# The opening of a two-model kernel: modulation blocks as columns on TensorE, three of them on VectorE, and a paired first projection

## The reference, cut to what matters

```python
s_c = jax.nn.silu(c)
s_cc = jax.nn.silu(c_ctx)[None]
ml = (s_c @ w_mod[i] + b_mod[i]).reshape(-1, 3, 3, D)       # shift, scale, gate of three stages
h = gated_residual(h, ml, 0, swiglu(ada_in(h, norm_g[i, 0], ml, 0), ffn_w_in[i, 0], ffn_w_out[i, 0]), 0.5)
...
mc = (s_cc @ w_mod[i] + b_mod[i]).reshape(-1, 3, 3, D)
hc = gated_residual(hc, mc, 0, swiglu(ada_in(hc, norm_g[i, 0], mc, 0), ffn_w_in[i, 0], ffn_w_out[i, 0]), 0.5)
```

## Time and profile before

| | |
|---|---|
| median of 3 runs | 3142.65 us (3140.11 to 3145.58) |
| the profiled execution | 3145.35 us |
| its span, first to last instruction | 3143.5 us |
| TensorE busy | 3055.1 us, 97% |
| VectorE busy | 1778.6 us, 57% |
| ScalarE busy | 1177.8 us, 37% |
| mean granted clock of TensorE | 0.982 |
| HBM read | 417.30 MB, 133 GB/s |

### The profile page before, as it was taken

How to read it: one execution, slowest core, us unless ns; L and a number is a source line. 1 busy time by engine, 2 the same in 40 slices (tenths; PEclk the granted TensorE clock), 3 DMA queues, 4 the chain that set the end, 5 groups by cost and what they waited for, 6 DMA issues and landing times. The chain is left out here.

```text
span 3143.5 us, 46965 instructions
## 1 busy us (share of the span) xinstructions
PE 3055.1 (97%) x19451; PEld 2711.1 (86%) x19451; DVE 1778.6 (57%) x3279; ACT 1177.8 (37%) x2025; POOL 86.6 (3%) x132
## 2 busy tenths in 40 slices
PE   7999999999999999999999998999999999999998
PEld 3788889888888888888888878999898999899998
DVE  1667675435449886653333544556656665656665
ACT  2322224333343222232222444444544544454443
POOL 1000000000000000000000110000001000001000
PEclk9899999999999999999999999999999999999999
DMA  9346543122135566632423332656335454435452
GB/s 279 95 144 184 144 148 105 51 88 94 61 94 162 168 201 184 184 94 74 114 79 98 99 100 75 191 169 191 107 115 181 151 185 132 138 98 168 148 183 87
DMA packets 509004, 421.46 MB, mean 134 GB/s; under 512 B 18234, under 2 KB 505962, under 8 KB 508792
## 3 DMA queue, kind: packets, MB, share of 16 engines
q1 hardware_dynamic: 505752, 412.33, 43.0%
q0 software_dynamic: 3040, 6.13, 0.8%
HBM read 417.30 MB, written 1.12 MB: 133 GB/s over the span
## 5 line engine op out<-in xcount | busy, mean ns | idle before, releaser
L1387 DVE TENSOR_TENSOR w_low<-raw,w_high 128x1024 fp32r<-128x1024 f32 (+2 forms) x720 | 762.8, 1101 | 327.0 <-ACT w_high L925 325.8
L925 ACT ACTIVATE w_high<-raw 128x1024 fp32r<-128x1024 f32 (+2 forms) x720 | 648.2, 949 | 613.3 <-PE gemm L2042 360.5
L2042 PE MATMUL gemm<-xh,w_high 128*128 128x512 f32 (+1 forms) x1904 | 689.1, 362 | 6.8 <-DVE xl L1425 6.2
L2042 PE MATMUL gemm<-xl,w_high 128*128 128x512 f32 (+1 forms) x1904 | 681.0, 358 | 0.0
L2042 PE MATMUL gemm<-xh,w_low 128*128 128x512 f32 (+1 forms) x1904 | 681.0, 358 | 0.0
L2042 PEld LDWEIGHTS gemm<-xh,w_high 128*128 128x128 f32 x1904 | 359.3, 189 | 67.4 <-DVE xl L1425 6.9
L2042 PEld LDWEIGHTS gemm<-xh,w_low 128*128 128x128 f32 x1904 | 359.2, 189 | 57.6
L2042 PEld LDWEIGHTS gemm<-xl,w_high 128*128 128x128 f32 x1904 | 359.6, 189 | 55.3 <-issue 0.2
L2042 PE MATMUL gemm<-yh,w_high 128*128 128x256 f32 x1216 | 354.0, 291 | 12.8 <-DVE yl L1450 7.1
L2042 PE MATMUL gemm<-yl,w_high 128*128 128x256 f32 x1216 | 347.1, 285 | 0.0
L2042 PE MATMUL gemm<-yh,w_low 128*128 128x256 f32 x1216 | 346.9, 285 | 0.0
(11 more groups left out here) (331 smaller groups left out, 4278.0 us busy)
## 6 DMA issues: line engine op xcount, KB each, us to landing
raw<-in_ffn_w_in SPq DMA_DIRECT2D x176, 512.0 KB, 5.2
raw<-in_w_mod SPq DMA_DIRECT2D x72, 1024.0 KB, 7.1
raw<-in_w_in SPq DMA_DIRECT2D x50, 1024.0 KB, 5.3
raw<-in_w_up SPq DMA_DIRECT2D x32, 1024.0 KB, 5.5
raw<-in_w_down SPq DMA_DIRECT2D x32, 1024.0 KB, 5.2
raw<-in_ffn_w_out SPq DMA_DIRECT2D x32, 768.0 KB, 4.4
raw<-in_ret_w_in SPq DMA_DIRECT2D x24, 1024.0 KB, 5.2
raw<-in_ffn_w_out SPq DMA_DIRECT2D x32, 640.0 KB, 4.1
```

The source lines that it names most:

```text
L925: act.activation(wh[i % SPL][:, a:b], raw[slot_of["w", i]][:, a:b], ACT.Copy).then_inc(w_high, 1)
L1387: dve.tensor_tensor(wl[slot][:, a:b], raw[slot][:, a:b], wh[i % SPL][:, a:b].bitcast(F32), ALU.subtract).then_inc(w_low, 1)
L2042: ins = pe.matmul(out, l_, r_, start=first and j == 0, stop=last and j == 2)
```

## The change

The first stage's twelve modulation blocks are done in another way, and the opening's work is put in another order.

- The order of loads becomes 0, 8, 1, 2, (x, ctx), 9, 3, 4, 10, 5, 6, 7, and block 11 goes between the weight blocks. `MOD0` is 8: blocks 0 to 7 are TensorE's, blocks 8, 9, 10 (the first part of the gate) are done in the opening by VectorE with `sum_mod`, block 11 too, during the first projection.
- TensorE's blocks are done as columns: the raw block's 128 x 128 parts are the stationary operand and silu(c), silu(c_ctx) the two moving columns, 16 matmuls a block. The rows, their copies by ScalarE and the turns are gone; VectorE takes eight pairs of columns and the bias in one instruction. The T5 product goes to another PSUM bank.
- On TensorE the order is blocks 0, 1, 2, T5 product, transposes of x, then blocks 3 to 7 with the three additions over partitions between them, then the sums of squares and the spread.
- ScalarE does the decay and lambda work before the copies of `h`, then the squares, then the high part of weight block 0, then the root.
- `scales(0)` and `gates(0)` are apart: the gate is made after `in000`.
- The first projection is `wide`.

```diff
-MOD0 = 12
+FIRST_MODS = (0, 8, 1, 2, 9, 3, 4, 10, 5, 6, 7)
+MOD1 = len(FIRST_MODS)
+MOD0 = MOD1 - 3
...
-        seq = [("m", b) for b in range(MOD0)]
+        seq = [("m", b) for b in FIRST_MODS]
         mod_after = {}
-        spans = ((G["in000"].s0, G["ret_qk0"].s0, MOD0, 36), (G["in010"].s0, G["in100"].s0, 36, 72))
+        spans = ((G["in000"].s0 + 3, G["ret_qk0"].s0, MOD1, 36), (G["in010"].s0, G["in100"].s0, 36, 72))
...
             act.activation(sc[:, :, 1], vecB[:, VB["c_ctx"]:VB["c_ctx"] + 8], ACT.Silu).then_inc(c_silu, 1)
-            for b in range(4):
-                act.wait_ge(chunk_mod, b + 1)
-                act.activation(mrow[:, b % 4, :], bank[b % 4][0:2, 0:WB], ACT.Copy).then_inc(mod_row, 1)
-            for c in range(DC):
-                act.wait_ge(x_turned, c + 1)
-                act.activation(h[:, c, :], aux[c % 4][:, :], ACT.Copy).then_inc(h_init, 1)
...
             act.activation(lam[:, 4:8], lam[:, 0:4], ACT.Exp).then_inc(lam_exp, 1)
-            for b in range(4, MOD0):
...
+            for c in range(DC):
+                act.wait_ge(x_turned, c + 1)
+                act.activation(h[:, c, :], aux[c % 4][:, :], ACT.Copy).then_inc(h_init, 1)
+            N = norms["n00"]
+            for c in range(DC):
+                square(N, c)
+            splits_upto(0)
+            roots(N)
+            highs(N, 0, 4)
+            splits_upto(1)
+            highs(N, 4)
...
+            def take_columns(q):
+
+                n = min(8, 2 * MOD0 - 8 * q)
+                dve.wait_ge(chunk_mod, 4 * q + n // 2)
+                dve.tensor_tensor(mod[:, 8 * q:8 * q + n, :], bank[q][:, 0:2 * n].rearrange("p (c v) -> p c v", v=2),
+                                  vecA[:, 8 * q:8 * q + n].unsqueeze(2).to_broadcast([P, n, 2]),
+                                  ALU.add).then_inc(mod_out, 1)
...
+            dve.wait_ge(c_silu, 2)
+            sum_mod(MOD0)
             dve.wait_ge(small_in, 80)
-            take_rows(0)
...
-            for q in range(1, MOD0 // 4):
-                take_rows(q)
...
-            coefficients(0)
+            dve.wait_ge(t5_g, 1)
+            dve.tensor_copy(gt5[:, :], bank[3][0:8, :]).then_inc(t5_row, 1)
+            sum_mod(MOD0 + 1)
+            take_mod(MOD0)
+            sum_mod(MOD0 + 2)
+            take_mod(MOD0 + 1)
+            for q in range(2):
+                take_columns(q)
+            dve.wait_ge(mod_out, 2)
+            dve.wait_ge(mod_taken, 2)
+            scales(0)
+            N = norms["n00"]
+            inverses(N)
+            steps = pieces_of(N)
+            splits_upto(0)
+            for _ in range(4):
+                next(steps)
+            splits_upto(1)
+            run(steps)
+            take_mod(MOD0 + 2)
...
                     run(gemm(f"in{l}{f}{s}"))
+                    if l + f + s == 0:
+                        take_mods(12)
+                        gates(0)
+                        dve.wait_ge(coef_ready, 1)
...
-                    for m in range(n, n + 4):
+                    for m in range(n, n + 4) if n else ():
                         wait_chunk_out(pe, m - 4)
...
+            def mod_columns(b):
+
+                slot = slot_of["m", b]
+                pe.wait_ge(raw_in[slot], value_of["m", b])
                 for j in range(2):
                     o = 4 * (b % 4) + 2 * j
-                    ins = pe.matmul(aux[q % 2][:, o:o + 2], mrow[:, b % 4, P * j:P * j + P], ident[0:2, 0:2],
-                                    start=True, stop=True)
...
+                    for k in range(DC):
+                        at = WB * k + P * j
+                        ins = pe.matmul(bank[b // 4][:, o:o + 2], raw[slot][:, at:at + P], sc[:, k, :], start=k == 0,
+                                        stop=k == DC - 1)
                 ins.then_inc(chunk_mod, 1)
...
-            for b in range(4):
-                mod_rows(b)
-                if b:
-                    mod_turn(b - 1)
-            mod_turn(3)
+            for b in range(3):
+                mod_columns(b)
             pe.wait_ge(pool_ready, 5)
             pe.wait_ge(small_in, 80)
-            pe.matmul(aux[3][0:8, :], tab[:, :], hot[:, :], start=True, stop=True).then_inc(t5_g, 1)
+            pe.matmul(bank[3][0:8, :], tab[:, :], hot[:, :], start=True, stop=True).then_inc(t5_g, 1)
             pe.wait_ge(x_in, 64)
...
             pe.wait_ge(h_init, 8)
-            for b in range(4, MOD0):
-                mod_rows(b)
...
+            add_partitions(MOD0)
+            mod_columns(3)
+            mod_columns(4)
+            add_partitions(MOD0 + 1)
+            mod_columns(5)
+            mod_columns(6)
+            add_partitions(MOD0 + 2)
+            mod_columns(7)
+            N = norms["n00"]
+            for c in range(DC):
+                mean_square(N, c)
+            spread(N)
+            pe.wait_ge(mod_out, 2)
+            pe.wait_ge(t5_row, 1)
...
-                        run(gemm(f"in{l}{f}{s}", normed(f"n{l}{j}"), wide=s == 0 and G[f"in{l}{f}{s}"].n0 > 0))
+                        run(gemm(f"in{l}{f}{s}", normed(f"n{l}{j}"), wide=s == 0))
```

More of the change, by code:

```diff
@@ L178, in program @@
                                ("gt5", [8, 512], F32), ("tab", [33, 8], F32),
-                               ("hot", [33, 512], F32), ("mrow", [2, 4, WB], F32)])[7:]
-        xrows, vrows, lamv, lamp, rpbp, gt5, tab, hot, mrow = xrows
+                               ("hot", [33, 512], F32)])[7:]
+        xrows, vrows, lamv, lamp, rpbp, gt5, tab, hot = xrows
         qr = xt
@@ L598, in program @@
         raw_in = [sem(f"raw_in{i}") for i in range(RAW)]
-        chunk_mod = sem("mod_row_in_psum")
-        mod_row = sem("mod_row")
-        mod_cols = sem("mod_cols")
+        chunk_mod = sem("mod_columns_in_psum")
         mod_out = sem("mod_out")
@@ L1167, in _ @@
             act.activation(lam[:, 4:8], lam[:, 0:4], ACT.Exp).then_inc(lam_exp, 1)
-            for b in range(4, MOD0):
[L1169 to L1172, removed]
+            for c in range(DC):
[9 more added lines that the diff above has]
+            highs(N, 4)
             def ffn(l, f, j):
-                if norms[f"n{l}{j}"]["halves"] == 1:
+                if norms[f"n{l}{j}"]["halves"] == 1 and l + f:
                     norm(f"n{l}{j}")
@@ L1179, in ffn @@
                     run(gemm(f"out{l}{f}{s}"))
-            splits_upto(1)
             act.wait_ge(rpb_out, 16)
@@ L1665, in attention, with scales @@
                 out_low(n - 1)
[L1667 to L1671, removed]
+            def take_columns(q):
[4 more added lines that the diff above has]
+                                  ALU.add).then_inc(mod_out, 1)
             def coefficients(i):
+                scales(i)
+                gates(i)
+            def scales(i):
                 m0 = NMOD * (i // 3) + 24 * (i % 3)
@@ L1679, in coefficients, with gates @@
                                                    op0=ALU.add, op1=ALU.mult))
+            def gates(i):
+                m0 = NMOD * (i // 3) + 24 * (i % 3)
                 w = 2 if i < 4 else 1
@@ L1694, in _ @@
             dve.wait_ge(gains_ready, 3)
+            dve.wait_ge(c_silu, 2)
+            sum_mod(MOD0)
             dve.wait_ge(small_in, 80)
-            take_rows(0)
-            dve.wait_ge(t5_g, 1)
-            dve.tensor_copy(gt5[:, :], aux[3][0:8, :]).then_inc(t5_row, 1)
             dve.wait_ge(cexp, 1)
@@ L1725, in _ @@
                 chain(dve.tensor_scalar(lamn[:, l:l + 1], lamn[:, l:l + 1], -LAM_INIT[l], None, ALU.add))
-            for q in range(1, MOD0 // 4):
-                take_rows(q)
-            dve.wait_ge(mod_out, MOD0 // 4)
-            for v in range(2):
-                chain(dve.tensor_tensor(mod[:, 0:2 * MOD0, v], mod[:, 0:2 * MOD0, v], vecA[:, 0:2 * MOD0], ALU.add))
-            coefficients(0)
+            dve.wait_ge(t5_g, 1)
[18 more added lines that the diff above has]
+            take_mod(MOD0 + 2)
             def ffn(l, f, j, last=True):
-                if norms[f"n{l}{j}"]["halves"] == 1:
+                if norms[f"n{l}{j}"]["halves"] == 1 and l + f:
                     norm(f"n{l}{j}")
@@ L1741, in factors, with take_mods @@
             def factors(b1, i0, i1):
+                take_mods(b1)
+                for i in range(i0, i1):
+                    coefficients(i)
+                dve.wait_ge(coef_ready, i1)
+            def take_mods(b1):
                 for b in range(MOD0 + len(taken), b1):
@@ L1745, in factors @@
                 dve.wait_ge(mod_taken, b1 - MOD0)
[L1746 to L1750, removed]
             dve.wait_ge(rpb_out, 16)
@@ L2272, in _ @@
             pe.wait_ge(c_silu, 2)
[L2274 to L2279, removed]
+            def mod_columns(b):
+                slot = slot_of["m", b]
+                pe.wait_ge(raw_in[slot], value_of["m", b])
                 for j in range(2):
                     o = 4 * (b % 4) + 2 * j
```

(29 more changed lines are left out.)

## The result

| | before | changed |
|---|---|---|
| median of 11 runs | 3142.92 us | 3152.62 us |
| lowest to highest | 3138.9 to 3148.8 | 3145.35 to 3157.56 |
| the profiled execution | 3145.35 us | 3150.37 us |
| its span | 3143.5 us | 3148.5 us |
| mean granted clock | 0.982 | 0.977 |

The ratio of the times is 1.0029, with a 95% interval of 1.0019 to 1.0039: the change makes the kernel slower by 9.7 us (6.0 to 12.3), three tenths of a per cent. The forecast was 3152.3.

The account below looks back on a forecast made before the run. TensorE, busy 3055.1 of 3143.5 us, was taken as the bound. First projection +13.7, pair -5.4 and +2.6, body +0.9 gave +11.8; less 2.2 for the clock, +9.6 on 3142.65: 3152.3 us, forecast 3149 to 3157, full range 3144.5 to 3158.5.

Parts of the forecast that it names:

- The price of a column block: TensorE's opening: 32 instructions a block at 0.213 us, 6.8 us at the low clock, against 4.07 as a row.
- the fall at 474.9: Trace of the kernel before: 24 one-moving-column instructions behind a dense projection; clock falls from 1.00 to 0.51, TensorE never idle.
- The start at the low pace: First TensorE work from 13.04 us: claimed to run at half pace, despite the page's clock of 1.00.
- The transposes wake the clock: T5 product and transposes of x: may raise the clock, saving nothing to 4.5 us; middle taken, -2.2.
- The chain to the first matmul: Opening through sums, root, split and low parts: first projection at 106.3 us, 13.7 later than 92.59, before the clock term.
- The overhang of ScalarE's split: Before the root: ScalarE's high part of weight block 0 delays it past TensorE's sums by 0.5 us.
- The pair: First projection, two groups together: -5.4 us of waiting for pieces, +2.6 for starting at the low clock.
- Covered work: Opening: VectorE's three summations and ScalarE's decay work end by about 51 us under TensorE's blocks and cost nothing.
- rival B: First projections, 217 to 280 us: VectorE starves TensorE, up to +5 us, about 3157; chance 0.08.
- Rival A: Opening: columns run at full clock, first matmul at 72 us, -22.6 us, total 3120; chance 0.12.
- The total: Whole kernel: +9.6 us, to 3152.3 us.
- the addition: Kernel body: one modulation block moves there from the opening, one addition over partitions more, +0.9 us.

Follow-up runs that it names:

- run 1: Changed kernel with the column blocks' moving operand widened from 2 to 128 columns, 126 of them zeros: 3124.55 us.
- run 2: Changed kernel with 64 moving columns in the column blocks instead of 2: 3147.7 us.
- run 3: Changed kernel with blocks 0 to 7 as rows with turns again, the rest as changed: 3127.91 us.
- run 4: Kernel before with its twelve opening blocks as columns with two moving columns, in the old order: 3172.2 us.
- run 6: Changed kernel with the first projection one group at a time, as before, instead of paired: 3154.04 us.
- run 8: Changed kernel with columns and first norm's sums padded to 128 moving columns, and the sums moved right behind the transposes of x: 3118.78 us.
- run 9: run 8 with the inverse ahead of block 10's sum on VectorE and the spread behind block 4: 3115.96 us.

## Why the prediction was right, step by step

- **The price of a column block**, 32 x 0.213 = 6.8 us: measured 6.86 (20.6/3) and 6.9 (13.8/2). That the sums of squares and the fall at 474.9 could be carried over to two moving columns is borne out by runs 1 to 4. The loss is therefore shown to be the clock's, not only argued: with the weight loads left alone and the moving side padded it goes.
- **The start at the low pace** held: 96 instructions at 0.214 from 13.97 on, while the profile gives a granted clock of 1.00 for these microseconds, in this and every other run. Ahead of the first fall that column cannot be read; the distance of the starts can.
- **The transposes wake the clock**: forecast -2.2 as the middle between nothing and -4.5. Measured by the rows above: transposes 6.31 for 7.0 (0.7), additions 1.05 for 1.84 (0.8), blocks 3 and 4 in 13.07 for 13.79 (0.7), 2.2 in all. The middle was a choice, not a reasoning, and it came out right by luck of when in the stretch the clock rose; in run 2 the transposes took 5.03 and the blocks behind them 11.45. By the Trainium skill ("TensorE: Matmul & The Clock Gate", "Part 4: PE-mode transpose") full clock does not engage for transposes. Here the transposes ran at the full clock in their second part (in run 2, 20 of them in the 2 us from 38 to 40), behind column blocks and the T5 product, so the measurement decides: these fp32 transposes do run at 2.4 GHz. What share of the rise is the T5 product's no run separates.
- **The chain to the first matmul**: forecast 106.3 less 2.2, and 0.9 for the later start, is 105.0; measured 104.34. Of the 0.7 between them, 0.5 lies in TensorE's list up to the end of the sums (94.9 for 95.4) and 0.2 behind it. The overhang of ScalarE's split (0.5) is there: the root is done 0.8 us behind the sums, where it was 0.3 before. Both low parts ahead of the pair are in the rows, and so is that the sums stand behind all blocks and are not early (81.13).
- **The pair**: -5.4 for the lost waiting, +2.6 for the low clock (5.3 us at half) are -2.8; the four chunks took 27.75 us before (92.59 to 120.34) and 25.03 now (104.34 to 129.37), so -2.7. With the later start that it brings little is left: taking the pair away costs 2.7 us by the trace and 1.4 by the medians (run 6).
- **Covered work**: VectorE's sums ended at 23.2, 43.3 and 50.7, the decay work at 28, and behind the first block TensorE waited for no load. VectorE is busy for 52.8 of 63 us in 217 to 280, against 50.0, and TensorE waits nowhere up to 480, so rival B is out.

```profile
217.00:280.00 63.00, 63.00 (x297) 51.83 (x296) 52.79 (x122) 12.88 (x19) 0.00 (x0) 1.00 0.49 159
```

- **Rival A** was nearly the right price for another kernel: its 3120, with the first projection at 72, compares with the 3124.6 and 75.35 of run 1, where the sums, left unpadded, took 11.1 us and not its 7.5. The rule that named it, in the Trainium skill ("TensorE: Matmul & The Clock Gate", "Why this matters for your kernels"), to keep TensorE busy without a break, does not hold for this form: busy without a gap from 44.3 to 81.1 us, TensorE is at 1.2 GHz for all but the first microsecond of it.
- **The total**, +9.6 against +9.7, is nearer than the parts deserve. By the rows of the profiles the parts are 10.8 for the first projection (11.75 less the late start; forecast 13.7 - 2.2 = 11.5), -2.7 for the pair and +0.8 for the addition: +8.9. A later row agrees: the last sums ahead of norm n01 begin at 486.42 instead of 474.97, 11.45 us later, of which 0.9 is the start and 1.7 a dip to 0.50 between 468 and 472 us that the kernel before does not have there; 8.8 is left. Single runs scatter by 12 us from lowest to highest and the interval of the difference reaches from 6.0 to 12.3, so the mechanism is confirmed, and the last tenths are luck.

What stays open: other widths of the column blocks than 2, 64 and 128 weren't tried, nor was the change with fewer or more blocks on VectorE.

## What to carry to other kernels

Before a product is turned round so that the large operand becomes the stationary one, look for a stretch of the trace with the same form, a full weight load for one or two moving columns, and read the clock there and just behind it: the price in that form may be twice that of the instruction count. If the form is wanted, try the moving side padded with zeros; to 128 columns that cost no time here (0.115 us an instruction, where one column takes about 0.12 at full clock; weight loads fill the stretch either way), and gave 28 us back. Sums over partitions with one column of ones are the same case (7.84 us for 64 in run 8, 13.79 in the changed kernel).

When work leaves one engine, ask what stood behind it in program order: the row copies cost TensorE little, but they held up ScalarE's splits and with them the sums, and an inverse left behind a 6 us summation took back 4.4 of the 10.8 us by which the first projection could start earlier (runs 8 and 9 against run 1).

## What was not expected of the hardware

- 128 moving columns behind a 128-column fp32 weight load cost no more than one: 7.39 us for 64 instructions, 0.115 each, at a granted clock of 1.00, against 0.95 for eight additions, 0.12 each, at the same clock.
- With 64 the clock stayed at 0.50 for blocks (5 to 7) that at 128 ran at 1.00 throughout.
- Behind a wait of 2.7 us (run 8) the clock was at 0.67 in 48 to 52 us, and without that wait (run 9) at 1.00 throughout. Behind waits of 1.06 and 0.56 us (run 1) it fell as well, but not behind one of 1.66 (runs 8 and 9, ahead of the sums). Each is one execution.
- The dips of the clock behind the opening are not the same in the two profiled executions, and one of them is worth 5 us, half of the effect studied. A single profile of each kernel would have shown 5.0 us for a difference of 9.7.
